# Three pairs in the first and sixth feed-forward stages of a two-block network, early block loads, and a buffer of its own for the last w_out chunk

## The chip, the cores and the metric

One core of a Trainium2 chip runs the whole kernel as one program. The metric is the device time of the execution in microseconds (us); three runs of the kernel before took 2106.66, 2107.87 and 2108.87 us, median 2107.87. Engines are called TensorE (PE in the rows), VectorE (DVE), ScalarE (ACT), GpSimd (POOL) and SyncE (SP, which here only issues DMAs).

## The reference, cut to what matters

One sequence of 256 tokens with 1024 features passes through four layers in float32: two of a first block (mixers HGRN2, then forgetting attention, "fox") and two of a second block (a short convolution, then sparse attention, "nsa", which has a shared key and value stage "kv" in front). Each layer has a feed-forward part before and one behind its mixer, so there are eight, called ffn 0 to ffn 7 here:

```
def swiglu(h, w_in, w_out):                  # w_in (1024, 2*2816), w_out (2816, 1024)
    gate, up = jnp.split(h @ w_in, 2, axis=-1)
    return (jax.nn.silu(gate) * up) @ w_out
x = x + 0.5 * swiglu(rmsnorm(x, g), w_in, w_out)
```

The order of stages is ffn 0, hgrn, ffn 1, ffn 2, fox, ffn 3, ffn 4, conv, ffn 5, kv, ffn 6, nsa, ffn 7.

## The kernel before, in words

*Splits.* Every float32 operand is split into a high and a low part in TensorE's fp32r type, and a product is three matmuls: high by high, high by low, low by high. ScalarE writes the high part (`w_hi`, `wo_hi`, `ht_hi`), VectorE the low one by a subtraction (`w_lo`, `wo_lo`, `ht_lo`). Each piece of weights (128 x 2048 values) goes through both, into a ring of four slots.

*A feed-forward stage.* It starts with the transposition of x (L653), scaled and split into `xt_hi_`, `xt_lo_`. The 2816 hidden features are cut into 11 chunks of 256 (NCH = 11). A plain chunk loads 512 columns of w_in (gate and up, 2 MB, into `raw_in`, L431), and TensorE makes `2 token tiles x 8 slices x 3 = 48` matmuls of 512 columns (L561 to L563). `read(t)` is the silu on ScalarE (L1149) and the gating on VectorE (L1310), which gives h. `turn(c)` transposes h on TensorE (L888) and splits it (`ht_hi`, `ht_lo`), `weights_out(c)` splits 1 MB of w_out (L1108, L1242) that came into `raw_out` (L435), and `second(c)` adds 24 matmuls (L907 to L909) into four PSUM banks. The last two chunks have code of their own (L965 to L967), with w_out split by halves (L1220, L1384).

*Pairs.* A pair takes chunks c and c+1 together by Strassen's scheme in Winograd's form: the 256 tokens x 1024 features by 1024 x 1024 product is seen as 2 x 2 blocks and made with seven products of 12 matmuls (L839 to L841) in place of eight, 84 matmuls for 96. The order is B11, B21, T2, T3, T1, B22, T4. `blocks` are four 1 MB blocks of w_in in the arena (b11, b12, b21, b22, L447); T3 is b12 + b22, made by an accumulating DMA that GpSimd issues (L1042) once b12 has landed; T2, T4 and T1 are sums on VectorE (L1024, L1028, L1033); `dve_x_add` makes four sums of x, which `act_x_sum` and `dve_x_sum` split (S1 to S4, L1050, L1057). The results are combined on VectorE: the gate of the first tile (L1251), p1s (L1271), `up0` (L1280), `up1` (L1287), p1s again (L1288), `up0` again (L1292), and so on. TensorE may start the pair's second product only when h of chunk c-1 has been read out of bank 1, and the plain chunk after a pair only when up0 has been made (L1292).

`PAIRED` says which chunks begin pairs: 4 and 7 in ffn 0; 2, 5 and 8 in ffn 1, 2, 3, 4 and 7; none in ffn 5 and 6.

*What sets the order.* Every engine has one instruction stream, written out by these functions; semaphores tie them. SyncE issues nearly all weight loads in one order: a plain chunk's load waits until the chunk before is split; w_out's load (`out`) waits until the last contents of `raw_out` are split; blocks of the next pair wait until the pair before has used theirs. Where the first pair of a stage follows a mixer (ffn 1, 3, 7), its blocks are asked for behind chunk 0's work, once the mixer's first x is there. In ffn 0 two blocks go behind chunk 1's turn, two behind chunk 2's.

*GpSimd.* Beside T3 it issues the loads of constants, and in ffn 5 it prepares kv: a bias table and compress weights are loaded (L2203 to L2217), the positions are summed (L2231 to L2238), kv0 is zeroed (L2219). In ffn 5's chunk 0 TensorE makes the bias rows (L2269), ScalarE copies and writes them (L2276, L2278). In ffn 6 hidden matmuls (L2324) read the compress weights, the last one also the positions; after it GpSimd loads the bias table (L2254).

## Time and profile before

| | us |
|---|---|
| median of three runs | 2107.87 |
| profiled execution | 2108.13 |
| its span | 2106.8 |
| TensorE busy in it | 2044.6 |
| VectorE, ScalarE busy | 1514.9, 1138.3 |

The profile is of one execution. The span is the time from its first to its last instruction. A matmul's duration is that of its passage through a pipeline, so that the next starts well before its end; how long a run of matmuls takes is read from starts. "Idle before" and a releaser stand in brackets behind a timeline row.

### The profile page before, as it was taken

Reading aid. Unit: us, or ns where it says so; the run is one execution under the profiler, and the core shown is the slowest. Engines: PE = TensorE matmul, PEld = TensorE weight load, DVE = VectorE, ACT = ScalarE, POOL = GpSimd, SP = SyncE. Lnnn points to the kernel's source line nnn. Section 1 sums busy time; section 2 is a strip of 40 time slices with the busy share of each in tenths; the row PEclk is TensorE's granted clock in tenths of the full one; section 3 lists DMA queues with packets and bytes.
Section 4 is the critical chain, followed back from the end, with each engine's and each line's share of the span. In section 5 each row is a group of like instructions: output and inputs, shape, how many; then the busy total and the mean of one; then the engine's idle time right before and its main releaser. Section 6 shows DMA issues by size and latency. Waiting matters only on the chain.

```text
span 2106.8 us, 26202 instructions
## 1 busy us (share of the span) xinstructions
PE 2044.6 (97%) x10287; PEld 1705.5 (81%) x10287; DVE 1514.9 (72%) x1777; ACT 1138.3 (54%) x1417; POOL 93.4 (4%) x130
## 2 busy tenths in 40 slices
PE   8999999999999999999999999999999999989999
...
PEclk9999999999999999999999999999999999999999
...
DMA packets 232955, 377.82 MB, mean 179 GB/s; under 512 B 18766, under 2 KB 129786, under 8 KB 232832
## 3 DMA queue, kind: packets, MB, share of 16 engines
...
q8 instruction: 82, 1.34, 0.3%
...
## 4 chain that ended last, share of the span: by engine, by line
PE 72%; DVE 13%; ACT 6%; DMA 5%; issue 4%; SPq 0%; DVEq 0%; ACTq 0%
PE bank L561 10%; PE bank L563 10%; PE bank L562 10%; PE acc L907 5%; PE acc L909 5%; PE acc L908 5%; DVE w_lo_ L586 3%; DMA raw_in<-ffn_w_in 2%; PE bank L556 2%; PE bank L557 2%; PE bank L558 2%; PE bank L839 2%; PE bank L840 2%; PE bank L841 2%; DMA raw_out<-ffn_w_out 2%
## 5 line engine op out<-in xcount | busy, mean ns | idle before, releaser
L586 DVE TENSOR_TENSOR w_lo_<-raw_in,w_hi_ 128x2048 fp32r<-128x2048 f32 (+1 forms) x265 | 418.6, 1589 | 137.2 <-ACT w_hi_ L576 136.8
L561 PE MATMUL bank<-w_hi_,xt_hi_ 128*128 128x512 f32 x1104 | 444.6, 403 | 6.6 <-DVE arena L1292 2.4
L563 PE MATMUL bank<-w_hi_,xt_lo_ 128*128 128x512 f32 x1104 | 431.4, 391 | 0.0
L562 PE MATMUL bank<-w_lo_,xt_hi_ 128*128 128x512 f32 x1104 | 430.2, 390 | 0.0
L576 ACT ACTIVATE w_hi_<-raw_in 128x2048 fp32r<-128x2048 f32 (+1 forms) x265 | 351.3, 1346 | 82.0 <-DMA raw_in<-ffn_w_in 32.1
L1242 DVE TENSOR_TENSOR wo_lo_<-raw_out,wo_hi_ 128x2048 fp32r<-128x2048 f32 x80 | 183.6, 2296 | 191.7 <-ACT wo_hi_ L1108 191.5
L1007 DVE TENSOR_TENSOR w_lo_<-arena,w_hi_ 128x2048 fp32r<-128x2048 f32 x119 | 270.4, 2285 | 9.0 <-ACT w_hi_ L999 9.0
L999 ACT ACTIVATE w_hi_<-arena 128x2048 fp32r<-128x2048 f32 x119 | 225.5, 1909 | 53.8 <-DVE arena L1033 28.8
L561 PEld LDWEIGHTS bank<-w_hi_,xt_hi_ 128*128 128x128 f32 x1104 | 207.6, 188 | 51.2 <-DVE arena L1292 5.0
L563 PEld LDWEIGHTS bank<-w_hi_,xt_lo_ 128*128 128x128 f32 x1104 | 207.2, 188 | 44.8
L562 PEld LDWEIGHTS bank<-w_lo_,xt_hi_ 128*128 128x128 f32 x1104 | 207.9, 188 | 38.1
L1108 ACT ACTIVATE wo_hi_<-raw_out 128x2048 fp32r<-128x2048 f32 x80 | 153.0, 1912 | 156.9 <-PE acc L909 124.2
L907 PE MATMUL acc<-wo_hi_,ht_hi_ 128*128 128x512 f32 x576 | 226.0, 392 | 3.8 <-DVE ht_lo_ L1237 3.8
L909 PE MATMUL acc<-wo_hi_,ht_lo_ 128*128 128x512 f32 x576 | 225.2, 391 | 0.0
L908 PE MATMUL acc<-wo_lo_,ht_hi_ 128*128 128x512 f32 x576 | 224.9, 390 | 0.0
L907 PEld LDWEIGHTS acc<-wo_hi_,ht_hi_ 128*128 128x128 f32 x576 | 108.6, 188 | 28.6 <-DVE ht_lo_ L1237 4.7
L909 PEld LDWEIGHTS acc<-wo_hi_,ht_lo_ 128*128 128x128 f32 x576 | 108.5, 188 | 22.9
L908 PEld LDWEIGHTS acc<-wo_lo_,ht_hi_ 128*128 128x128 f32 x576 | 108.5, 188 | 22.3
L1149 ACT ACTIVATE silu_<-bank,rstd_ 128x256 f32<-128x256 f32 x108 | 51.1, 473 | 134.7 <-PE bank L563 134.6
L1103 ACT ACTIVATE ht_hi_<-tr 128x512 fp32r<-128x512 f32 x80 | 47.6, 595 | 131.7 <-PE tr L888 113.7
L556 PE MATMUL bank<-xt_hi_,w_hi_ 128*128 128x256 f32 x352 | 101.9, 289 | 2.8 <-DVE xt_lo_ L747 2.8
L557 PE MATMUL bank<-xt_lo_,w_hi_ 128*128 128x256 f32 x352 | 99.6, 283 | 0.0
...
## 6 DMA issues: line engine op xcount, KB each, us to landing
...
arena<-ffn_w_in POOLq DMA_DIRECT2D x17, 1024.0 KB, 14.2
...
```

The source lines that it names most:

```text
L561: mm(o, xt_hi[:, k, tok], wh(k)[:, 0:w], start=first, stop=False)
L562: mm(o, xt_hi[:, k, tok], wl(k)[:, 0:w], start=False, stop=False)
L563: last = mm(o, xt_lo[:, k, tok], wh(k)[:, 0:w], start=False, stop=end)
L576: act.e.activation(g.piece(g.wh, n, half, k), raw, ACT.Copy).then_inc(g.w_hi, 4 if k is None else 1)
L586: dve.e.tensor_tensor(g.piece(g.wl, n, half, k), raw, g.piece(g.wh, n, half, k).bitcast(F32), ALU.subtract).then_inc(g.w_lo, 4 if k is Non ...
L907: mm(o, g.hth[:, at, :], g.oh[:, i, cols], start=(c == 0 and i == 0), stop=False)
L908: mm(o, g.hth[:, at, :], g.ol[:, i, cols], start=False, stop=False)
L909: ins = mm(o, g.htl[:, at, :], g.oh[:, i, cols], start=False, stop=False)
L999: act.e.activation(g.wh[:, op % 4], g.block_of(i), ACT.Copy).then_inc(g.w_hi, 4)
L1007: dve.e.tensor_tensor(g.wl[:, op % 4], g.block_of(i), g.wh[:, op % 4].bitcast(F32), ALU.subtract).then_inc(g.w_lo, 4)
L1108: act.e.activation(g.oh[:], g.raw_out[:], ACT.Copy).then_inc(g.wo_hi, 2)
L1242: dve.e.tensor_tensor(g.ol[:], g.raw_out[:], g.oh[:].bitcast(F32), ALU.subtract).then_inc(g.wo_lo, 2)
```

## The change

The diff changes seven things. (1) `PAIRED` gives ffn 0 three pairs, at 2, 5 and 8, and ffn 5 too. (2) In ffn 0 all four blocks of the first pair are asked for right behind chunk 1's load and w_out's chunk 0. (3) For ffn 7 they are asked for in nsa. (4) The last w_out chunk of each paired stage but ffn 5 goes to a buffer of its own, `raw_last` in the arena, asked for when the last pair's sixth product is done; the next load into `raw_out` no longer waits for it. (5) In a stage's first pair S3's and S1's splits on VectorE move into the chunk before, T1's sum goes ahead of T3's split, and in every pair the split of the next chunk's second half goes behind up0. (6) ffn 7's B11 is split before chunk 0's w_out, as in the others. (7) GpSimd's preparations for kv move behind ffn 5's last pair, the zeroing of kv0 ahead of the positions; the bias rows are made in kv. The memset of hgrn's scores waits for ffn 0's end.

```diff
...
-PAIRED = {f: (2, 5, 8) if f else (4, 7) for f in (0, 1, 2, 3, 4, 7)}
+PAIRED = {f: (2, 5, 8) for f in (0, 1, 2, 3, 4, 5, 7)}
 PAIRS = [(f, c) for f in range(8) for c in PAIRED.get(f, ())]
...
     return f * NCH + c + (f >= 3) + (f >= 7)
+ASIDE = [m_of(f, NCH - 1) for f in PAIRED if f != 5]
+def outs_until(m):
+    return m + 1 - len([a for a in ASIDE if a <= m])
...
         self.up1 = self.masks[:].rearrange("p a b -> p (a b)")[:, 0:CW].bitcast(F32)
+        self.raw_last = self.area(10240, FC // P, D)
         self.silu0 = self.silu_[:].rearrange("p a b -> p (a b)")
+    def last_out(self, f):
+        return self.raw_last if m_of(f, NCH - 1) in ASIDE else self.raw_out
...
     def out(m, dst, src):
-        sp.wait_ge(g.wo_lo, 2 * m)
+        sp.wait_ge(g.wo_lo, 2 * (m - (m - 1 in ASIDE)))
         sp.e.dma_start(dst, src).then_inc(g.landed_out, 16)
...
             def w_out_chunk(c):
+                if m_of(f, c) in ASIDE:
+                    sp.wait_ge(g.prod, PDN[N0[s] + PAIRED[f][-1]] + 6)
+                    sp.e.dma_start(g.raw_last, w_out[c]).then_inc(g.last_in, 16)
+                    return
                 if f == 7 and c == 0:
...
                     chunk(i)
-                if here and f == 0 and c in (1, 2):
-                    for which in ((1, 0), (2, 3))[c - 1]:
+                if here and PAIRED.get(f, (0,))[0] == 4 and c in (1, 2):
+                    for which in ((1,), (0, 2, 3))[c - 1]:
                         block(p, which)
                     todo = 1
-                    if here:
+                    if here and not f:
+                        for which in (1, 0, 2, 3):
+                            block(p, which)
+                    elif here and STAGES[s - 1] != "nsa":
                         sp.wait_ge(g.x_new, 4 * X[s - 1] + 1)
...
             chunk(i)
+        if kind == "nsa":
+            sp.wait_ge(g.ns_ob, NSA_HEADS)
+            for which in (2, 3):
+                block(p, which)
+            sp.wait_ge(g.xt_lo, 16 * U_NSA_O + 16)
+            for which in (1, 0):
+                block(p, which)
     o = g.t["out"].rearrange("o (t p) d -> p (o t) d", p=P)
...
     def weights_out(c):
-        act.wait_ge(g.landed_out, 16 * (m_of(f, c) + 1))
+        act.wait_ge(g.landed_out, 16 * outs_until(m_of(f, c)))
         used_out(c)
...
             p = PAIRS.index((f, c + 1))
-            if before != "S" and f != 7:
+            if before != "S":
                 act_block(g, act, p, B11)
...
                 turn(c - 1)
-                if f == 7:
-                    act_block(g, act, p, B11)
                 act_block(g, act, p, B21)
...
         act.wait_ge(g.second, 20 * f + 18 + i + 1)
-        act.wait_ge(g.landed_out, 16 * (m_of(f, c) + 1))
-        act.e.activation(g.oh[:, i], g.raw_out[:, i], ACT.Copy).then_inc(g.wo_hi, 1)
+        if m_of(f, c) in ASIDE:
+            act.wait_ge(g.last_in, 16 * (ASIDE.index(m_of(f, c)) + 1))
+        else:
+            act.wait_ge(g.landed_out, 16 * outs_until(m_of(f, c)))
+        act.e.activation(g.oh[:, i], g.last_out(f)[:, i], ACT.Copy).then_inc(g.wo_hi, 1)
         act.wait_ge(g.h_turned, 12 * f + c + i + 1)
...
         if first_one:
+            dve_block_sum(g, dve, p, T1)
             dve_block(g, dve, p, T3)
-            dve_block_sum(g, dve, p, T1)
             gate0()
-            dve_x_sum(g, dve, f, A_S3)
-            dve_x_sum(g, dve, f, A_S1)
         else:
...
         dve.e.tensor_tensor(g.p1s, y[:], g.p1s, ALU.add).then_inc(g.st_c, 1)
-        dve_split(g, dve, n + 2, 1)
         dve.wait_ge(g.prod, PDN[n] + 6)
         dve.e.scalar_tensor_tensor(g.up0, a[:], -1.0, g.up0, ALU.mult, ALU.subtract).then_inc(g.st_c, 1)
+        dve_split(g, dve, n + 2, 1)
         dve.wait_ge(g.silu, 22 * f + 2 * c + 2)
...
                 dve_x_sum(g, dve, f, A_S2)
-                if f != 7:
-                    dve_block(g, dve, p, B11)
+                dve_block(g, dve, p, B11)
                 weights_out(c - 1)
+                dve_x_sum(g, dve, f, A_S3)
                 read(0)
                 turn(c - 1)
-                if f == 7:
-                    dve_block(g, dve, p, B11)
                 dve_block(g, dve, p, B21)
+                dve_x_sum(g, dve, f, A_S1)
                 read(1)
+                dve_block_sum(g, dve, p, T3)
                 dve_block_sum(g, dve, p, T2)
...
         dve.wait_ge(g.wo_hi, 2 * m_of(f, c) + i + 1)
-        dve.e.tensor_tensor(g.ol[:, i], g.raw_out[:, i], g.oh[:, i].bitcast(F32), ALU.subtract).then_inc(g.wo_lo, 1)
+        dve.e.tensor_tensor(g.ol[:, i], g.last_out(f)[:, i], g.oh[:, i].bitcast(F32), ALU.subtract).then_inc(g.wo_lo, 1)
         dve.wait_ge(g.ht_hi, 12 * f + c + i + 1)
...
     pool.e.dma_start(g.masks[:], g.t["c_masks"]).then_inc(g.masks_in, 16)
+    pool.wait_ge(g.wo_lo, 2 * NCH)
     pool.e.memset(g.hg_scores[:], 0.0).then_inc(g.hg_zero, 1)
...
     t = g.t
-    for i in range(4):
-        pool.wait_ge(g.x_new, 4 * X[S_FFN[5] - 1] + i + 1)
+    pool.wait_ge(g.prod, PDN[N0[S_FFN[5]] + PAIRED[5][-1]] + 7)
     pool.e.dma_start(g.relb[0:N_BUCKETS], t["rel_bias_2"]).then_inc(g.rel_in, 16)
...
     for kv, w in enumerate((t["cmp_w1_k_2"], t["cmp_w1_v_2"])):
-        pool.wait_ge(g.prod, PDN[N0[S_FFN[5]] + 3 + kv])
         pool.e.dma_start(g.w1[kv * DH:(kv + 1) * DH], w.rearrange("(j d) h -> d j h", d=DH)).then_inc(g.compress_in, 16)
         pool.e.dma_start(g.w2[:, kv], w).then_inc(g.compress_in, 16)
+    pool.e.memset(g.kv0, 0.0).then_inc(g.kv_set, 1)
+    pool.wait_ge(g.kv_set, 6)
+    pool.e.memset(g.vv.rearrange("p a b g d -> p (a b g) d")[:, :, DH:], 1.0).then_inc(g.kv_set, 1)
+    pool.wait_ge(g.kv_set, 7)
     pool_positions(g, pool)
-    pool.e.memset(g.kv0, 0.0).then_inc(g.kv_set, 1)
-    pool.wait_ge(g.kv_set, 7)
-    pool.e.memset(g.vv.rearrange("p a b g d -> p (a b g) d")[:, :, DH:], 1.0).then_inc(g.kv_set, 1)
...
-def pe_bias_slot(g, pe, j):
+def pe_bias(g, pe):
     rb = g.relb[0:REL_ROWS]
-    if j == 8:
-        pe.wait_ge(g.rel_in, 32)
-        pe.wait_ge(g.kv_set, 1)
-        pe.e.matmul(g.accs[0][0:NSA_HEADS, :], rb, g.onehot[0:REL_ROWS], start=True,
-                    stop=True).then_inc(g.kv_rows_mm, 1)
-def act_bias_slot(g, act, j):
-    if j == 8:
-        act.wait_ge(g.kv_rows_mm, 1)
-        act.e.activation(g.rows[0:NSA_HEADS], g.accs[0][0:NSA_HEADS, :], ACT.Copy).then_inc(g.kv_rows, 1)
-        act.wait_ge(g.kv_rows, 1)
-        act.e.dma_start(g.bias_rows.rearrange("c h w -> h c w"),
-                        g.rows[0:NSA_HEADS].unsqueeze(1).to_broadcast([NSA_HEADS, COPIES, REL_W])).then_inc(g.bias_wrote, 16)
+    pe.wait_ge(g.rel_in, 32)
+    pe.wait_ge(g.kv_set, 1)
+    pe.e.matmul(g.accs[0][0:NSA_HEADS, :], rb, g.onehot[0:REL_ROWS], start=True, stop=True).then_inc(g.kv_rows_mm, 1)
+def act_bias(g, act):
+    act.wait_ge(g.kv_rows_mm, 1)
+    act.e.activation(g.rows[0:NSA_HEADS], g.accs[0][0:NSA_HEADS, :], ACT.Copy).then_inc(g.kv_rows, 1)
+    act.wait_ge(g.kv_rows, 1)
+    act.e.dma_start(g.bias_rows.rearrange("c h w -> h c w"),
+                    g.rows[0:NSA_HEADS].unsqueeze(1).to_broadcast([NSA_HEADS, COPIES, REL_W])).then_inc(g.bias_wrote, 16)
...
             j = 2 * (c - 1) + t
+            if (c, t) == (1, 0):
+                pe_bias(g, pe)
             if c == 1:
...
     if i == CMP_BLOCK - 1:
-        pe.wait_ge(g.kv_set, 6)
+        pe.wait_ge(g.kv_set, 8)
         pe.e.matmul(g.accs[3][:, 0:2], g.pe_sum, g.pe_half, start=True, stop=True)
...
                 return
+            if j == 0:
+                act_bias(g, act)
             if j == 3:
...
```

## Rows read from the trace of the kernel before

**Rows 1.** The page: busy time by engine, granted clock in tenths.
```profile
PE 2044.6 (97%) x10287; PEld 1705.5 (81%) x10287; DVE 1514.9 (72%) x1777; ACT 1138.3 (54%) x1417; POOL 93.4 (4%) x130
...
PEclk9999999999999999999999999999999999999999
```

**Rows 2.** Waits of TensorE: us in total, times, longest.
```profile
PE acc L907 <- DVE ht_lo_ L1237: 3.8, 2, 2.1
...
PE acc L965 <- DVE ht_lo_ L1387: 2.8, 6, 1.2
...
PE bank L839 <- DVE silu_ L1251: 2.5, 1, 2.5
PE bank L561 <- DVE arena L1292: 2.4, 6, 0.4
```

**Rows 3.** TensorE timeline, edges of ffn 1 and ffn 5 (start, us, instruction).
```profile
357.63 1.04 PE L653 MATMUL tr<-ident,x_tok 128*128 128x128 f32 x8
540.82 1.03 PE L653 MATMUL tr<-ident,x_tok 128*128 128x128 f32 x8
1350.43 1.03 PE L653 MATMUL tr<-ident,x_tok 128*128 128x128 f32 x8
1359.21 1.03 PE L2269 MATMUL acc<-arena 33*16 33x512 f32 x2
1539.57 0.39 PE L967 MATMUL acc<-wo_hi_,ht_lo_ 128*128 128x512 f32 x1
```

**Rows 4.** Timeline, first pair of ffn 1, TensorE and VectorE.
```profile
403.44 0.48 PE L839 MATMUL bank<-w_hi_,sums_split 128*128 128x512 f32 x1 [0.35 <-DVE w_lo_ L1007]
414.41 0.68 DVE L1292 SCALAR_TENSOR_TENSOR arena<-bank,arena 128x512 f32<-128x512 f32 x1
415.15 0.50 PE L561 MATMUL bank<-w_hi_,xt_hi_ 128*128 128x512 f32 x1 [0.40 <-DVE arena L1292]
```

**Rows 5.** TensorE timeline, last chunks of ffn 1 and ffn 2.
```profile
535.24 0.50 PE L965 MATMUL acc<-wo_hi_,ht_hi_ 128*128 128x512 f32 x1 [0.50 <-DVE ht_lo_ L1387]
...
719.13 0.50 PE L965 MATMUL acc<-wo_hi_,ht_hi_ 128*128 128x512 f32 x1 [1.18 <-DVE ht_lo_ L1387]
```

**Rows 6.** Opening: timeline, windows (busy us, clock, DMA), landings of L447, L1042.
```profile
29.66 0.47 ACT L1149 ACTIVATE silu_<-bank,rstd_ 128x256 f32<-128x256 f32 x1
56.78 0.50 PE L907 MATMUL acc<-wo_hi_,ht_hi_ 128*128 128x512 f32 x1 [1.72 <-DVE ht_lo_ L1237]
...
20.00:25.00 5.00, 5.00 (x24) 3.81 (x22) 4.90 (x9) 4.97 (x9) 0.00 (x0) 1.00 0.74 283
...
35.00:40.00 5.00, 5.00 (x24) 4.14 (x23) 5.00 (x5) 2.25 (x2) 1.34 (x1) 1.00 1.04 386
...
DMA to landing us min/median/max: 5.1/7.7/19.8
...
DMA to landing us min/median/max: 12.2/14.2/14.9
```

**Rows 7.** ffn 7's first pair: timeline, and the window behind the stop.
```profile
1946.59 2.29 DVE L1024 TENSOR_TENSOR arena<-arena 128x2048 f32<-128x2048 f32 x1 [2.76 <-DMA arena<-ffn_w_in]
1959.18 0.77 PE L839 MATMUL bank<-w_hi_,sums_split 128*128 128x512 f32 x1 [2.51 <-DVE silu_ L1251]
...
1959.20:1962.20 3.00, 3.00 (x7) 2.42 (x8) 2.69 (x3) 3.00 (x3) 0.00 (x0) 0.50 0.03 5
```

**Rows 8.** GpSimd's timeline; VectorE's splits in 1423:1467 and in 1500:1535.
```profile
1423.12 0.61 POOL L2231 TENSOR_TENSOR arena<-arena,gains 128x256 f32<-128x256 f32 x1 [9.53 <-DMA arena<-cmp_w_v]
...
1464.57 1.82 POOL L2219 MEMSET arena<- 128x2048 f32 x1
1603.72 4.52 POOL L2254 DMA_DIRECT2D arena<-bias_rows  x8 [137.14 <-PE acc L2324]
...
L586 DVE TENSOR_TENSOR w_lo_<-raw_in,w_hi_ 128x2048 fp32r<-128x2048 f32 x5 | 12.4, 2475 | 2.5 <-ACT w_hi_ L576 2.5
...
L586 DVE TENSOR_TENSOR w_lo_<-raw_in,w_hi_ 128x2048 fp32r<-128x2048 f32 x4 | 9.2, 2288 | 2.0 <-ACT w_hi_ L576 2.0
```

More of the change, by code:

```diff
@@ L161 @@
 ns_csub ns_cexp ns_cp ns_cturned ns_cpt ns_cpv ns_co ns_turned13
-b11_in b12_in b21_in b22_in t3_in st_add st_t3 sa_raw ss_hi ss_lo st_cp st_c masks_in
+last_in b11_in b12_in b21_in b22_in t3_in st_add st_t3 sa_raw ss_hi ss_lo st_cp st_c masks_in
 own_act own_dve own_pool
@@ L335, in kv_views @@
         self.kv0 = self.area(8768, CMP_STRIDE, 2 * GROUPS, T // CMP_STRIDE)
-        self.pe_w1 = [self.area(8768, 2, P), self.area(9792, 2, P)]
+        self.pe_w1 = [self.area(13120, 2, P), self.area(13376, 2, P)]
         self.pe_sum = self.area(10816, P)
@@ L891, in second @@
     def second(c):
-        if c == 0 and f == 5:
+        if c == 0 and f == 6:
             pe.wait_ge(g.kv_rows, 1)
-        elif c == 0 and f == 6:
             pe.wait_ge(g.kv_gelu, 2)
@@ L1970, in act_narrow @@
 def act_narrow(g, act, m, w, f, hi):
-    act.wait_ge(g.landed_out, 16 * (m + 1))
+    act.wait_ge(g.landed_out, 16 * outs_until(m))
     act.wait_ge(g.acc, 4 * f)
@@ L2241, in pool_positions @@
     ins.then_inc(g.kv_set, 1)
-    pool.wait_ge(g.kv_set, 6)
+    pool.wait_ge(g.kv_set, 8)
 def pool_cmp_bias(g, pool):
@@ L3077, in pe_program @@
     pe_conv(g, pe)
-    pe_ffn(g, pe, 5, lambda j: pe_bias_slot(g, pe, j))
+    pe_ffn(g, pe, 5)
     pe_kv(g, pe)
@@ L3094, in act_program @@
     act_conv(g, act)
-    act_ffn(g, act, 5, lambda j: act_bias_slot(g, act, j))
+    act_ffn(g, act, 5)
     act_kv(g, act)
@@ L3113, in dve_program @@
     dve_conv(g, dve)
-    dve_ffn(g, dve, 5, lambda j: None)
+    dve_ffn(g, dve, 5)
     dve_kv(g, dve)
@@ L3130, in pool_program @@
     pool_conv(g, pool)
+    pool_pairs(g, pool, 5)
     pool_kv(g, pool)
```

## The prediction

> **What bounds the kernel now.** I read the page first: TensorE is busy 97% of the span, and its granted clock stands at full nearly everywhere [rows 1]. So time is won only by giving TensorE fewer matmuls, or by closing its few gaps. Second, the table of TensorE's waits [rows 2]: they add up to some 63 us in the whole run, and those that lie in feed-forward stages are small and repeated: six on ht_lo at L1387 (2.8 us, the stage ends), six on the arena at L1292 (2.4 us, the first plain chunk after a stage's first pair), one of 2.5 us on silu_. Third, the timeline at the stage edges, for what a pair is worth [rows 3]. Fourth, close views of one first pair, of two stage ends, of the opening 60 us, of the last stage, and of GpSimd around the kv stage [rows 4 to 8].
>
> **What a pair is worth.** Two plain chunks take 2 x 48 matmuls of 512 columns, a pair 7 x 12 = 84; it saves 12. A run of 24 such matmuls takes 540.82 - 535.24 = 5.58 us [rows 3, 5], 0.2325 us each, so 12 are 2.8 us. (The 0.39 us beside each matmul is its pipelined duration, not its pitch.) The stages show what is left of that. ffn 1, with three pairs, runs from 357.63 to 540.82: 183.2 us. ffn 5, with none, from 1350.43 to 1539.57 + 0.23: 189.4 us, of which the bias matmul at L2269 takes 1.0 (start 1359.21, next product 1360.17): 188.4 bare [rows 3]. ffn 1 holds three gaps of TensorE: 0.35, 0.40 and 0.50 us of idle [rows 4, 5], with slower restarts some 0.5 to 0.6 each, 1.6 together: 181.6 bare. The difference is 6.8 us, 2.3 per pair.
>
> **ffn 5 and kv.** ffn 5 gets three pairs and starts behind a mixer as ffn 1 does (blocks asked for when its x is there). I take ffn 1's bare 181.6, add 0.5 at its end (its last w_out chunk still goes through raw_out) and 0.4 for the wait that I expect in the first pair (next part): 182.5. That is 6.9 less than now. The bias matmul, its copy and the table's write move into kv: +1.0 there, as TensorE works without large gaps in kv. GpSimd's preparations (rel_bias, compress weights, positions) move from the stage's start to behind the last pair's seventh product. After that TensorE has six runs of 24 matmuls, about 33 us, to the stage's end E. GpSimd needs about 5 us to issue; the second compress load made it idle 9.5 us before the first position product, two loads in a row perhaps 21; the positions took 1423.12 to 1464.57, 41.5 us [rows 8]. They end at E - 33 + 5 + 21 + 41 = E + 34. The step that needs them (last hidden matmul) let GpSimd's next load go at 1603.72, E + 64. 30 us of slack hide it; the zeroing of kv0, now ahead of the positions, is ready long before kv. Value taken: 0.
>
> **First pairs, new order on VectorE.** In ffn 1 the sixth product waited (403.44, on w_lo of B22) and the next plain chunk waited (415.15, on up0, which stood at 414.41 behind the 2.28 us split of that chunk's second half) [rows 4]. S3 and S1 (0.68 each) now run in the chunk before, where VectorE idles for ScalarE and TensorE (0.8 and 1.2 us by the timeline), so everything up to B22 comes 1.2 to 1.3 us earlier: w_lo of B22 at 402.0 instead of 403.3, wanted at 402.9. That wait goes. What is late next is T4: up0 must see the fifth product (ends 402.9, VectorE some 0.2 later), 0.68 us, then w_lo of T4, 2.28 us: 406.0, wanted at 405.7. T4 started at about 406.3 before; I book 0.15 us. The second wait goes whole, since up0 is now ahead of the split: 0.56 with its restart. The split then ends at about 415, and its half is read 2.7 us after the chunk's start at 414.6: hidden. 0.7 us per stage, four stages (ffn 1 to 4): -2.8. Bounds: 0 (T4 late by all that B22 gains) and 1.1 each.
>
> **Stage ends.** The last w_out chunk waits today for raw_out, which chunk 9 frees late; ScalarE's copy then holds back ht_hi and ht_lo: 0.50 in ffn 1, 1.18 in ffn 2 [rows 5], 2.8 in six stages [rows 2]. In its own buffer, asked for after the last pair, it lands over 10 us early, and the chain copy 1.06, ht_hi 0.37, ht_lo 0.42 fits beside 12 matmuls. ffn 1 to 4: -2.4; -0.2 each in ffn 0 and ffn 7 is in their sums.
>
> **ffn 7.** T3, the sum that GpSimd's accumulating DMA makes, landed at 1946.59 after VectorE idled 2.76 us for it; TensorE then stopped 2.51 us at 1959.18 and ran at half clock (0.50 granted, 1.2 GHz, after that stop) over the next matmuls [rows 7]: 12 of them took 4.3 us instead of 2.8. With the first pair's blocks asked for during nsa (from about 1900 and 1907), T3 is there near 1925, needed at 1943. Gone: idle 2.5, 0.4, 0.3, 0.4 and 0.2 (that at the end), 1.5 of half clock, 0.7 of restarts: 6.0. ffn 7 has 1 us less room than ffn 1 in front of T2, so I leave 0.2 for T4: -5.8. Bounds -4 and -6.5. The 0.8 on h_tok at its second chunk stays.
>
> **ffn 0.** One pair more: -2.3. Its wait of 1.72 us at 56.78 (chunk 2 landed late behind blocks) goes with its cause, 1.9 with restart [rows 6]; the two first-pair waits and the end as above: -1.3. Against that stands a first pair that comes 35 us earlier. Data: from 20 to 25 us the DMA moved 283 GB/s at a share of 0.74 [rows 6], because the queue ran dry near 24. The blocks, 1 MB each, now queue there: at 380 GB/s 2.8 us each, b12 at 27, b11 at 30, b21 at 33, b22 at 36; T3 is issued at 28 and takes 12.2 to 14.9 us [rows 6]: 41 to 43. ScalarE must now make the four x sums (0.57 each) before the second silu of chunk 0, which ended its wait at 29.66: it comes 2.2 to 2.6 us later, h at 32.9, and TensorE, wanting it at 32.2, waits 0.8. Then ScalarE is free for B11 at 32.3, after the landing. VectorE: B11 to 36.6, w_out 38.8, S3, h, ht_lo 40.5, B21 42.7, S1, second h 43.8. TensorE is done with B11 at 41.6 and may not overwrite the bank before that h: 2.3 us. Then T2 sum, T4 sum and T2's split end at 50.5, wanted at 52.4; B22's at 61.3, wanted 60.8: 0.6; T4 0.2. Together +3.9. Sum of the stage: -2.3 - 1.9 - 1.3 + 3.9 = -1.6. Bounds: no new wait, -5.5; b11 landing after 19.8 us, the slowest of these loads [rows 6], at 38: +6 more, +4.5.
>
> **Sum.** -1.6 (ffn 0) - 2.8 - 2.4 (ffn 1 to 4) - 6.9 (ffn 5) + 1.0 (kv) - 5.8 (ffn 7) = -18.5. The profiled execution took 2108.13 us (span 2106.8), 0.3 above the median 2107.87. 2108.1 - 18.5 = 2089.6 us.
>
> **A rule that speaks against it.** While GpSimd computed the positions, VectorE's splits took 2475 ns on average, against 2288 without it [rows 8]: 0.2 us each, and some ten such operations will meet it in kv and ffn 6, mostly with slack. The Trainium skill (SBUF — State Buffer, "Who interferes with whom") says that a VectorE instruction with two SBUF inputs and a GpSimd instruction that reads SBUF exclude each other, and the later one blocks for the whole instruction. By the row's average the move costs 0 to 2 us, by the rule it can be the price of the fourth rival below.
>
> **Rivals.**
> - *The opening starves.* For it: the DMA is full from 35 us on (386 GB/s) [rows 6] and plain chunk 4's 2 MB now queue beside T3. Against: 6 MB in 17 us are within the rate seen. b11 or T3 6 us late, paid one for one by an idle TensorE: 2089.6 + 6.4 = 2096.
> - *The opening is covered.* VectorE keeps up and ScalarE's x sums fit: 3.9 us of waits shrink to none: 2085.7.
> - *The first pairs gain nothing.* T4 inherits all of B22's wait and later products the chunk's: 2.8 lost in ffn 1 to 4, and 0.9, 0.7 and 0.9 in ffn 0, 5 and 7: 2094.9. For it: VectorE has no idle left from T2's sum to the last split. Against: up0 ahead of the split needs nothing that is late.
> - *GpSimd in the way.* Each of kv's six splits on VectorE waits for one whole position product of 0.61 us [rows 8], and TensorE with it: 3.7 us more, 2093.3. For it: the 2475 ns. Against: that row shows a third of it, and in kv VectorE idles over a microsecond before most splits.
> - *Slower: the positions come too late.* One chain, the compress loads behind three pairs' traffic and then 41.5 us of positions, ends after E + 64. It decides when the loads take over 50 us, and eats the whole gain at 69 us: 2108 and above. For it: it starts some 90 us later in the stage than today. Against: 9.5 us of idle today [rows 8], 14.9 the slowest accumulate.
>
> **Chances.** Forecast 0.62 (own range 2086 to 2093), starved opening 0.12, covered opening 0.12, GpSimd 0.06, first pairs 0.05, late positions 0.03. This kernel's runs lie within 0.1% of each other; 0.2% is what I call no change, 4.2 us. Faster 0.96, same 0.01, slower 0.03. The range of 8 in 10 reaches down to the covered and up to the starved opening: 2085 to 2096.5.
>
> **What would show it.** ffn 5 at 182 to 183 us with 84 matmuls of L839 to L841 per pair; no wait on silu_ in ffn 7, its clock at full; no wait on up0 after first pairs, a small one at the seventh product; none on ht_lo at L1387 except in ffn 5; in ffn 0 a wait of about 2 us at the second product of the first pair, on h. It is wrong if TensorE idles over 6 us between 30 and 70 us, if the hidden matmul waits for kv_set, or if kv grows by over 2 us.

## The result

The changed kernel takes 2095.11 us, the median of 4 runs (2094.11 to 2098.04), against 2108.37 us (2106.66 to 2109.81) for the kernel before in the same session: ratio 0.994, 95% interval [0.9922, 0.9957]. It is faster, and 5.5 us slower than the 2089.6 us forecast, near the upper end of the range. One stage missed by more than that: ffn 5 was to become 6.9 us shorter and became 3.2 us longer, 10.1 us off. Gains elsewhere that no term foresaw hid some of it.

The stages of the profiled executions, each from its first transposition of x to that of the next stage (ffn 7 to the end of its last matmul), in us:

| stage | before | after | predicted | measured |
|---|---|---|---|---|
| ffn 0 | 192.48 | 190.91 | -1.6 | -1.57 |
| ffn 1 to 4 | 737.03 | 730.94 | -5.2 | -6.09 |
| fox | 158.85 | 157.80 | 0 | -1.05 |
| ffn 5 | 191.31 | 194.52 | -6.9 | **+3.21** |
| kv | 32.81 | 33.84 | +1.0 | +1.03 |
| ffn 6 | 212.00 | 209.37 | 0 | -2.63 |
| nsa | 127.40 | 128.26 | 0 | +0.86 |
| ffn 7 | 190.02 | 184.11 | -5.8 | -5.91 |

hgrn and conv did not move (0.01 each), and x arrives 0.3 us earlier. The sum is -12.5, the difference of the spans 2106.8 and 2094.3.

### The profile after

The page's first block and its clock row; they answer to [rows 1]. TensorE shows 48 matmuls fewer, four more pairs of 12 each, and still 97%.

```profile
PE 2035.0 (97%) x10239; PEld 1699.0 (81%) x10239; DVE 1583.3 (76%) x1823; ACT 1162.5 (56%) x1423; POOL 90.3 (4%) x134
...
PEclk9999999999999999999999999999999999989999
```

TensorE's waits (us in total, times, longest), as in [rows 2]. The six waits on ht_lo at stage ends, the six on the arena behind first pairs and the one on silu_ are gone. In their place stand seven on w_lo, one in each stage's first pair, 0.3 at the most, two on h_tok in ffn 0 (1.7, and 0.56 on another line), and one of 7.6 us that no term of the forecast has. The 0.7 on h_tok at L587 is the one in ffn 7 that was to stay.

```profile
PE acc L990 <- DVE ht_lo_ L1263: 7.6, 1, 7.6
...
PE tr L865 <- DVE w_lo_ L1032: 1.9, 7, 0.3
PE bank L865 <- DVE h_tok L1334: 1.7, 1, 1.7
...
PE acc L932 <- DVE ht_lo_ L1263: 1.0, 1, 1.0
PE bank L587 <- DVE h_tok L1334: 0.7, 1, 0.7
```

The timeline of that place, several engines (start, us, instruction; SPq and POOL's DMA rows are issues). Read it from the bottom up. TensorE stops for 7.57 us because VectorE's ht_lo is late; VectorE stands behind its own split of the out weights, that behind ScalarE's copy at 1514.66, and the copy behind the load of out weights 9. Their buffer was free at 1500.25 (1497.96 + 2.29). SyncE was then still issuing w_kv, 16 loads that took it until 1502.8; ScalarE could copy the load behind them at 1514.66, 11.8 us after its issue. GpSimd had asked for 2 MB of compress weights at 1492.55 and 1493.67.

```profile
1486.93 15.85 SPq L443 DMA_DIRECT2D raw_in<-w_kv  x16
1502.83 16.75 SPq L447 DMA_DIRECT2D raw_out<-ffn_w_out  x2
1492.55 1.13 POOL L2238 DMA_DIRECT2D arena<-cmp_w_k  x1 [0.53 <-POOL arena L2235]
1493.67 1.09 POOL L2238 DMA_DIRECT2D arena<-cmp_w_v  x1
1497.96 2.29 DVE L1268 TENSOR_TENSOR wo_lo_<-raw_out,wo_hi_ 128x2048 fp32r<-128x2048 f32 x1 [1.19 <-ACT wo_hi_ L1133]
1514.66 1.91 ACT L1133 ACTIVATE wo_hi_<-raw_out 128x2048 fp32r<-128x2048 f32 x1 [13.26 <-DMA raw_out<-ffn_w_out]
1519.83 0.80 PE L990 MATMUL acc<-wo_hi_,ht_hi_ 128*128 128x512 f32 x1 [7.57 <-DVE ht_lo_ L1263]
```

The same stretch in windows (busy time of PE, PEld, DVE, ACT, POOL, then granted clock, DMA share, GB/s). The DMA engines are busy all the time from 1500 to 1510 and move 183 GB/s, where [rows 6] have 386 at a like share. Behind the stop TensorE runs partly at its lower level, 1.2 GHz: the 12 matmuls from 1519.83 take 5.3 us, where 12 take 2.8 at 2.4 GHz. 7.6 and 2.5 make the 10.1 by which the stage missed its forecast.

```profile
1500.00:1510.00 10.00, 10.00 (x47) 8.26 (x47) 2.85 (x3) 0.48 (x1) 0.00 (x0) 1.00 1.13 183
1510.00:1520.00 10.00, 2.43 (x11) 1.70 (x10) 3.33 (x3) 4.56 (x4) 7.99 (x12) 0.74 0.35 116
1520.00:1530.00 10.00, 10.00 (x36) 7.89 (x37) 5.08 (x5) 3.03 (x5) 9.06 (x13) 0.75 0.85 315
```

The stage edges, which answer to [rows 3]: ffn 1 from 355.73 to 537.73, ffn 5 from 1341.38 to 1535.90.

```profile
355.73 1.04 PE L679 MATMUL tr<-ident,x_tok 128*128 128x128 f32 x8
537.73 1.04 PE L679 MATMUL tr<-ident,x_tok 128*128 128x128 f32 x8
1341.38 1.03 PE L679 MATMUL tr<-ident,x_tok 128*128 128x128 f32 x8
1535.90 2.02 PE L677 MATMUL tr<-diag_,x_tok 128*128 128x128 f32 x16 [1.90 <-DVE diag_ L770]
```

### The profile page after: what moved, and what is told of

It reads as the page before. It is cut to its first block, busy times and chain, and to the rows that moved or that the text cites. A ratio compares the mean times of both kernels' runs of the same rounds, so it can differ in the third digit from the quotient of the medians.

```text
span 2094.3 us, 26216 instructions
## 1 busy us (share of the span) xinstructions
PE 2035.0 (97%) x10239; PEld 1699.0 (81%) x10239; DVE 1583.3 (76%) x1823; ACT 1162.5 (56%) x1423; POOL 90.3 (4%) x134
## 3 DMA queue, kind: packets, MB, share of 16 engines
HBM read 378.72 MB, written 1.57 MB: 182 GB/s over the span
## 4 chain that ended last, share of the span: by engine, by line
PE 82%; DVE 9%; ACT 4%; issue 2%; DMA 2%; SPq 1%; DVEq 0%; ACTq 0%
PE bank L587 9%; PE bank L589 9%; PE bank L588 9%; PE acc L932 6%; PE acc L934 6%; PE acc L933 6%; PE bank L866 3%; PE bank L865 3%; PE bank L867 3%; PE tr L865 3%; PE tr L866 3%; PE tr L867 3%; PE bank L582 2%; PE bank L583 2%; PE bank L584 2%
## 5 line engine op out<-in xcount | busy, mean ns | idle before, releaser
L612 DVE TENSOR_TENSOR w_lo_<-raw_in,w_hi_ 128x2048 fp32r<-128x2048 f32 (+1 forms) x243 | 380.8, 1575 | 119.5 <-ACT w_hi_ L602 119.2
L587 PE MATMUL bank<-w_hi_,xt_hi_ 128*128 128x512 f32 x976 | 394.2, 404 | 3.2 <-DVE xt_lo_ L713 2.4
L589 PE MATMUL bank<-w_hi_,xt_lo_ 128*128 128x512 f32 x976 | 382.1, 391 | 0.0
L588 PE MATMUL bank<-w_lo_,xt_hi_ 128*128 128x512 f32 x976 | 380.9, 390 | 0.0
L602 ACT ACTIVATE w_hi_<-raw_in 128x2048 fp32r<-128x2048 f32 (+1 forms) x243 | 320.1, 1338 | 77.8 <-DMA raw_in<-ffn_w_in 24.0
L1032 DVE TENSOR_TENSOR w_lo_<-arena,w_hi_ 128x2048 fp32r<-128x2048 f32 x147 | 334.5, 2284 | 5.6 <-ACT w_hi_ L1024 5.6
L1024 ACT ACTIVATE w_hi_<-arena 128x2048 fp32r<-128x2048 f32 x147 | 278.8, 1910 | 56.4 <-DVE arena L1049 29.5
L587 PEld LDWEIGHTS bank<-w_hi_,xt_hi_ 128*128 128x128 f32 x976 | 184.0, 189 | 40.0 <-issue 4.8
L589 PEld LDWEIGHTS bank<-w_hi_,xt_lo_ 128*128 128x128 f32 x976 | 183.5, 188 | 39.8
L865 PE MATMUL bank<-w_hi_,sums_split 128*128 128x512 f32 x252 | 100.6, 399 | 0.2 <-DVE silu_ L1277 0.2
L866 PE MATMUL bank<-w_lo_,sums_split 128*128 128x512 f32 x252 | 100.3, 398 | 0.0
```

What stands on the lines that cost most here:

```text
L587: mm(o, xt_hi[:, k, tok], wh(k)[:, 0:w], start=first, stop=False)
L588: mm(o, xt_hi[:, k, tok], wl(k)[:, 0:w], start=False, stop=False)
L589: last = mm(o, xt_lo[:, k, tok], wh(k)[:, 0:w], start=False, stop=end)
L602: act.e.activation(g.piece(g.wh, n, half, k), raw, ACT.Copy).then_inc(g.w_hi, 4 if k is None else 1)
L612: dve.e.tensor_tensor(g.piece(g.wl, n, half, k), raw, g.piece(g.wh, n, half, k).bitcast(F32), ALU.subtract).then_inc(g.w_lo, 4 if k is Non ...
L865: mm(bank[:], hi[:, k], wh[:, k], start=k == 0, stop=False)
```

## The experiments

"Out weights 9" and "10" are the w_out pieces of ffn 5's last two chunks; a load lands when its data can be used. Two theories for ffn 5. **A**: GpSimd's two compress loads, which the change moved behind the last pair, hold back the out weights. **B**: the 16 small-row loads of w_kv ahead of them in SyncE's queue do it. All edits are made on the changed kernel. The stages that moved, from each run's one profiled execution, and the median of the runs that were repeated (e5 to e8 ran once). ffn 5 with the collision as it is took 193.47, 193.91 and 194.52 us in three executions (e5, e8, after), so that a difference of less than 1 us in this stage says nothing:

| run | ffn 0 | ffn 1 | ffn 2 | ffn 3 | ffn 4 | fox | ffn 5 | ffn 6 | nsa | ffn 7 | kernel |
|---|---|---|---|---|---|---|---|---|---|---|---|
| before | 192.48 | 183.19 | 185.83 | 183.04 | 184.97 | 158.85 | 191.31 | 212.00 | 127.40 | 190.02 | 2108.37 |
| after | 190.91 | 182.00 | 183.60 | 181.63 | 183.71 | 157.80 | 194.52 | 209.37 | 128.26 | 184.11 | 2095.11 |
| e1 compress late | 190.41 | 181.76 | 183.58 | 181.64 | 184.09 | 157.77 | 198.15 | 209.55 | 128.40 | 184.06 | 2099.14 |
| e2 out between kv | 190.22 | 181.62 | 183.57 | 181.64 | 183.59 | 157.79 | 191.78 | 209.84 | 128.44 | 184.18 | 2093.55 |
| e3 both | 190.42 | 181.89 | 183.55 | 181.62 | 183.61 | 156.15 | 198.04 | 209.48 | 128.48 | 184.13 | 2099.43 |
| e4 two pairs | 189.96 | 181.94 | 183.60 | 181.61 | 183.73 | 157.82 | 186.91 | 208.40 | 130.79 | 184.07 | 2088.61 |
| e9 compress last | 190.30 | 181.66 | 183.57 | 181.64 | 183.58 | 156.20 | 184.08 | 208.85 | 128.30 | 184.10 | 2083.81 |
| e9 again | 190.71 | 181.68 | 183.61 | 181.65 | 183.56 | 156.23 | 184.21 | 208.12 | 128.57 | 184.13 | 2085.54 |
| e11 long rows | 190.32 | 181.69 | 183.63 | 181.60 | 183.63 | 157.78 | 193.95 | 208.99 | 128.59 | 184.06 | 2093.84 |
| e5 ffn 0 (4, 7) | 189.87 | 181.86 | 183.59 | 181.63 | 185.03 | 159.63 | 193.47 | 209.54 | 127.31 | 184.13 | |
| e10: e9 and e5 | 189.58 | 181.62 | 183.55 | 181.64 | 183.64 | 158.70 | 184.22 | 208.94 | 127.29 | 184.24 | 2084.82 |
| e6 no own buffer | 191.24 | 182.46 | 184.11 | 182.19 | 184.81 | 157.82 | 195.15 | 209.46 | 128.40 | 184.70 | |
| e7 old order | 191.75 | 182.49 | 184.41 | 182.47 | 184.44 | 157.48 | 195.35 | 208.08 | 128.80 | 184.90 | |
| e8 ffn 7 late | 190.22 | 182.36 | 183.57 | 181.63 | 184.16 | 157.74 | 193.91 | 209.43 | 128.60 | 189.12 | |

### e1: the compress loads behind out weights 9

```diff
     pool.wait_ge(g.kv_set, 5)
+    pool.wait_ge(g.landed_out, 16 * outs_until(m_of(5, NCH - 2)))
     for kv, w in enumerate((t["cmp_w1_k_2"], t["cmp_w1_v_2"])):
```

> GpSimd starts the two 1 MB compress loads only when chunk 9 of ffn 5's out weights has landed; nothing else is changed. ffn 5 took 194.5 us with a TensorE wait of 7.6 us. Theory A (the compress loads hold the rings, w_kv's small rows alone do not): the 16 w_kv loads are issued in about 9 us instead of 15.9, out weights 9 are asked for at about 1500.3 instead of 1502.8 and land in 5 to 6 us instead of 11.7, the wait falls below 1 us, and with the clock's restart gone ffn 5 takes 184.5 to 185.5 and the kernel about 2085.5. Theory B (the 16 w_kv loads ahead in the same queue do it): the issue still ends near 1502.8 and the landing stays above 8 us, the wait stays at 5 us or more, ffn 5 takes 191 or more, the kernel 2092 or more. Both by halves: a wait of 3 to 4, ffn 5 near 189.

2099.14 us, ratio to before 0.9947 [0.9932, 0.9962]: no better than the changed kernel's 0.994 [0.9922, 0.9957], and neither theory's number. ffn 5 takes 198.15, 3.6 us more. Its timeline:

```profile
1487.13 9.19 SPq L443 DMA_DIRECT2D raw_in<-w_kv  x16
1500.47 10.95 SPq L447 DMA_DIRECT2D raw_out<-ffn_w_out  x2
1507.44 1.13 POOL L2239 DMA_DIRECT2D arena<-cmp_w_k  x1 [15.22 <-DMA raw_out<-ffn_w_out]
1506.71 1.92 ACT L1133 ACTIVATE wo_hi_<-raw_out 128x2048 fp32r<-128x2048 f32 x1 [5.12 <-DMA raw_out<-ffn_w_out]
1526.05 1.06 ACT L1246 ACTIVATE wo_hi_<-raw_out 128x1024 fp32r<-128x1024 f32 x1 [13.10 <-DMA raw_out<-ffn_w_out]
1529.20 0.80 PE L990 MATMUL acc<-wo_hi_,ht_hi_ 128*128 128x512 f32 x1 [10.83 <-DVE ht_lo_ L1411]
```

Every step of A came true for out weights 9: w_kv is issued in 9.19 us, the load is asked for at 1500.47 and lands at 1506.7, and TensorE does not wait for it. But the compress loads, now sent at 1507.44, met the next load of the same kind, out weights 10, asked for at about 1511: it landed after some 15 us and TensorE stopped for 10.83. Ahead of that load stood only the compress loads, w_kv's small ones were long through: A's mechanism is shown, and its sum was wrong, because I looked at one load and not at the next.

### e2: out weights 9 between the halves of w_kv

```diff
-    def chunk(i):
+    def chunk(i, halves=(0, 1)):
...
-        for half in range(2):
+        for half in halves:
...
+                if before == "S" and (f, c) == (5, NCH - 1):
+                    chunk(i, (0,))
+                    w_out_chunk(c - 1)
+                    chunk(i, (1,))
+                    todo = c
+                    continue
                 if before == "S":
                     chunk(i)
```

> In SyncE's program the load of out weights 9 of ffn 5 goes between the two halves of w_kv instead of behind both; GpSimd's compress loads stay where they are. Theory A (compress loads): out weights 9 are asked for at 1500.3 at the earliest, since their buffer is free only then, and still share the engines with what is left of 2 MB of compress loads: landing in 8 us or more, a wait of 3 to 5 us, ffn 5 at 188 to 191. Theory B (w_kv): with one half of w_kv behind it the load lands in about 5 to 6 us, wait below 1, ffn 5 at 184.5 to 185.5, the kernel about 2085.5.

2093.55 us, 0.9919 [0.9904, 0.9934]. ffn 5 at 191.78, a wait of 5.52. Timeline:

```profile
1498.68 0.37 SPq L447 DMA_DIRECT2D raw_out<-ffn_w_out  x1
1511.23 1.91 ACT L1139 ACTIVATE wo_hi_<-raw_out 128x2048 fp32r<-128x2048 f32 x1 [11.41 <-DMA raw_out<-ffn_w_out]
1516.19 0.80 PE L996 MATMUL acc<-wo_hi_,ht_hi_ 128*128 128x512 f32 x1 [5.52 <-DVE ht_lo_ L1269]
```

The load is asked for as soon as its buffer is free and still takes 12.5 us to land. So the place in SyncE's queue is worth some 2 to 3 us of the stage (by the kernel's ratio it can't be told), and B as the main cause is out: it wanted a landing of 5 to 6 us and a wait below 1. The other half of w_kv, asked for just behind, shared the engines with the load all the same.

### e3: both edits

The two edits above together.

> Both edits together. Either theory: out weights 9 land by 1506, no wait over 1 us, ffn 5 at 184.4 (the value predicted without the collision) to 185.5, the kernel 2085 to 2086. If ffn 5 stays above 187, neither queue order nor the compress loads are the whole cause, and the third pair itself costs something that was not counted.

2099.43 us, 0.9947 [0.9933, 0.9962]; ffn 5 at 198.04. Both theories' forecast failed, for e1's reason: ScalarE's copy of out weights 9 starts at 1504.03, and that of out weights 10 waits 13.81 us for its load.

### e4: two pairs in ffn 5

```diff
-PAIRED = {f: (2, 5, 8) for f in (0, 1, 2, 3, 4, 5, 7)}
+PAIRED = {f: (2, 5) if f == 5 else (2, 5, 8) for f in (0, 1, 2, 3, 4, 5, 7)}
```

> ffn 5 with pairs on chunks 2 and 5 only; chunks 8 to 10 as plain chunks; the compress loads follow the second pair. The collision goes (those loads are out about 50 us earlier, w_kv is asked for behind plain chunks), and one pair's gain of about 2.3 us goes with it. Collision as the whole cause: ffn 5 at 186.5 to 187.5, the kernel 2087 to 2088, faster than the kernel with three pairs. If pairs in this stage were themselves dear: ffn 5 below 185.5.

2088.61 us, 0.9895 [0.9878, 0.9911]. ffn 5 takes 186.91, as forecast from the collision as the whole cause (186.5 to 187.5). The collision itself did not go: out weights asked for at 1450.55, in a stretch without w_kv, land 14 us later beside the compress loads. TensorE does not wait for them; there was room.

```profile
1465.06 1.92 ACT L1133 ACTIVATE wo_hi_<-raw_out 128x2048 fp32r<-128x2048 f32 x1 [1.09 <-DMA raw_out<-ffn_w_out]
```

The run also shows what the third pair is worth in this stage: 186.91 less e9's 184.08 and 184.21 is 2.7 to 2.8, nearly all of its 12 matmuls. The mean of all three there is less, 2.1: the stage before without its bias matmul (190.3) against 184.1.

### e9: the compress loads behind the stage's last out weights

```diff
-    pool.wait_ge(g.landed_out, 16 * outs_until(m_of(5, NCH - 2)))
+    pool.wait_ge(g.landed_out, 16 * outs_until(m_of(5, NCH - 1)))
```

(against e1: one load later.)

> GpSimd starts the two 1 MB compress loads only when ffn 5's last out weights (chunk 10) have landed; nothing else is changed against the changed kernel. If the compress loads beside a wanted out-weights load are the whole cause: both landings take 5 to 6 us again, no wait over 1.5 us on ht_lo in this stage, ffn 5 at 184.4 to 185.5, the kernel about 2085 to 2086, some 10 us below the changed one. The loads are then out at about 1532 and the positions at about 1565, wanted near 1587: no new wait in ffn 6. Rival: the loads now meet w_kv's later chunks (1 MB each, wanted in kv) and kv pays what ffn 5 gains: kv at 40 or more, the kernel near 2092. Second rival: the third pair is dear by itself, ffn 5 above 187.

2083.81 us, 0.9889 [0.9873, 0.9906]. Timeline:

```profile
1484.02 9.15 SPq L443 DMA_DIRECT2D raw_in<-w_kv  x16
1497.36 0.37 SPq L447 DMA_DIRECT2D raw_out<-ffn_w_out  x1
1507.87 0.37 SPq L447 DMA_DIRECT2D raw_out<-ffn_w_out  x1
1513.55 1.13 POOL L2239 DMA_DIRECT2D arena<-cmp_w_k  x1 [24.44 <-DMA raw_out<-ffn_w_out]
1586.31 4.51 POOL L2279 DMA_DIRECT2D arena<-bias_rows  x8 [15.29 <-PE acc L2348]
```

ffn 5 takes 184.08 us, 0.3 from the 184.4 that my terms gave, and kv stays at 33.96, so that the rival that kv pays for it (40 or more) is out, and so is that of a dear third pair (above 187): the two w_kv loads asked for just ahead of the compress loads, 1 MB each, land in time. The positions end 15.29 us before the hidden matmul lets GpSimd go on; the changed kernel had 54.49 us there, so the loads can't go much later. That closes the case: where the 2 MB lie decides 10 us.

> The compress loads behind ffn 5's last out weights, once more, beside the variant with two pairs in ffn 0 and on its chip: 2083 to 2085, ffn 5 at 184.1. fox at 156.2 or 157.8: if it takes different values from run to run of one kernel, its gain against the kernel before belongs to the granted clock and not to the change.

2085.54 us, 0.9885 [0.987, 0.9899]. This is the version that beats both kernels: by some 10 us the changed one, by 1.1% the kernel before.

### e11: the same bytes in long rows

The weights arrive in another order, so this kernel's result is another one; it serves for the time alone.

```diff
-        pool.e.dma_start(g.w1[kv * DH:(kv + 1) * DH], w.rearrange("(j d) h -> d j h", d=DH)).then_inc(g.compress_in, 16)
+        pool.e.dma_start(g.w1[kv * DH:(kv + 1) * DH], w.rearrange("(d j) h -> d j h", d=DH)).then_inc(g.compress_in, 16)
```

> The two compress loads stay where the changed kernel has them, move the same 2 x 1 MB, but read 16 KB in one piece per partition instead of 32 rows of 512 bytes; the weights so arrive in another order, so the compressed keys and values are other numbers (their use takes the same instructions). Theory 1 (short rows: the engines are busy all the time and move only 180 to 230 GB/s): the two loads land in 5 to 7 us, w_kv is issued in about 9 us again, out weights 9 are asked for at 1500.5 and land in 5 to 6 us, the wait of 7.6 us falls below 1, ffn 5 at 184 to 185.5, the kernel near 2084 to 2086. Theory 2 (2 MB more on the rings, whatever the rows, or the two queues against each other): landing of out weights 9 stays above 8 us, ffn 5 at 189 or more.

2093.84 us, 0.9925 [0.9909, 0.9942]. ffn 5 at 193.95, wait 5.91. Timeline:

```profile
1507.25 10.37 SPq L447 DMA_DIRECT2D raw_out<-ffn_w_out  x2
1512.88 1.91 ACT L1133 ACTIVATE wo_hi_<-raw_out 128x2048 fp32r<-128x2048 f32 x1 [11.77 <-DMA raw_out<-ffn_w_out]
```

193.95 lies among the three executions of the unchanged stage: the row length of the compress loads is no main cause, as theory 2 has it, though its landing (above 8 us) did not come. The delay only moved from the landing to the issue: w_kv kept SyncE until 1507.2, and the load behind it then landed in 5.6 us. In this slot 2 MB of GpSimd's and 2 MB of w_kv were asked for together, ahead of 1 MB that was wanted soon. Between 1487 and the landing 5 MB went through in 26 us here and in 28 in the changed kernel. w_kv alone is slow as well: in e1 its 2 MB kept the engines busy from 1487 to about 1498, some 200 GB/s. So are the compress loads: window of e9 in which nothing else moves (180 GB/s at full engines).

```profile
1520.00:1526.00 6.00, 4.21 (x31) 3.62 (x30) 3.46 (x10) 3.73 (x11) 0.00 (x0) 1.00 1.04 180
```

What makes them slow, if not their rows, no run here tells.

### e5 and e10: ffn 0 with pairs on chunks 4 and 7

```diff
-PAIRED = {f: (2, 5, 8) for f in (0, 1, 2, 3, 4, 5, 7)}
+PAIRED = {f: (2, 5, 8) if f else (4, 7) for f in (0, 1, 2, 3, 4, 5, 7)}
```

> ffn 0 alone goes back to two pairs, on chunks 4 and 7, its first pair's blocks asked for behind chunks 1 and 2 as in the kernel before; all else as in the changed kernel. By the prediction's terms that stage without its third pair and without the opening's new waits, but with the new order and its own last buffer: -1.3 against 192.5, so 191.2, perhaps 189.3 if the old wait at the third chunk (1.9) was due to the order of the blocks. Theory 1 (the third pair pays 1.6 net): 191.5 to 192.5. Theory 2 (the opening's waits eat all of the pair's 2.3): 190 to 191, no difference to the changed kernel's 190.2 to 190.9.

> The compress loads behind ffn 5's last out weights, and ffn 0 with two pairs on chunks 4 and 7. ffn 0 at 189.9 (against 190.3 with three pairs), ffn 5 at 184.1, the kernel 2083 to 2084.5: level with the version that has three pairs in ffn 0, if the third pair is eaten by the opening's waits; 1.5 us or more slower if the third pair pays there.

Theory 2. TensorE timeline of e5, the edges of ffn 0:

```profile
9.21 1.97 PE L679 MATMUL tr<-ident,x_tok 128*128 128x128 f32 x8 [3.18 <-DMA x_tok<-x]
...
199.08 1.13 PE L677 MATMUL tr<-diag_,x_tok 128*128 128x128 f32 x8 [1.78 <-DVE diag_ L770]
```

189.87 us, and 189.58 in e10, against 189.96 to 190.91 with three pairs in nine runs: the third pair in ffn 0 brings nothing, or loses some tenths. The opening is not quite that of the kernel before: SyncE asks for one block behind chunk 1 and three behind chunk 2, where it was two and two, and the old wait of 1.72 us is gone here too. e10 takes 2084.82 us, 0.9883 [0.9868, 0.9897], level with e9 beside it (2085.54).

### e6, e7, e8: one part undone each

One execution each; ffn 1 differs by up to 0.4 us between executions of the same code (181.62 to 182.00).

```diff
-ASIDE = [m_of(f, NCH - 1) for f in PAIRED if f != 5]
+ASIDE = []
```

> The last chunk's out weights go through raw_out again in every ffn stage; all else as in the changed kernel. Theory 1 (its own buffer took away the stage-end waits): ffn 1 +0.5, ffn 2 +1.1, ffn 3 and 4 +0.5 each, ffn 0 and 7 +0.2 to 0.4, and six waits on ht_lo at the stage ends come back. Theory 2 (the gain of ffn 1 to 4 is all the first pairs' new order): less than 0.3 in each stage. fox, which gained 1.0 that was not foreseen, stays at 157.8 if that was the clock's phase, and goes back to 158.9 if it hangs on the buffer.

Theory 1: the waits at stage ends are back (row below), and ffn 1, 2, 3 and 7 are longer by 0.46, 0.51, 0.56 and 0.59; ffn 4 by 1.10, but that stage also varies between 183.6 and 185.0 elsewhere (e5, before). fox stays at 157.82.

```profile
PE acc L990 <- DVE ht_lo_ L1411: 2.2, 6, 0.5
```

```diff
         if first_one:
+            dve_block(g, dve, p, T3)
             dve_block_sum(g, dve, p, T1)
-            dve_block(g, dve, p, T3)
             gate0()
+            dve_x_sum(g, dve, f, A_S3)
+            dve_x_sum(g, dve, f, A_S1)
...
+        dve_split(g, dve, n + 2, 1)
         dve.wait_ge(g.prod, PDN[n] + 6)
...
-        dve_split(g, dve, n + 2, 1)
...
-                dve_x_sum(g, dve, f, A_S3)
...
-                dve_x_sum(g, dve, f, A_S1)
...
-                dve_block_sum(g, dve, p, T3)
...
```

(The last line changes nothing: T3's sum is GpSimd's in every pair.)

> VectorE's order in and ahead of first pairs as in the kernel before (S3 and S1 inside the pair, T3's split ahead of T1's sum, the last split ahead of up0); all else as in the changed kernel. Theory 1 (the prediction: 0.7 us per first pair): ffn 1, 3 and 4 at +0.5 to +0.9 each, a wait of 0.3 to 0.4 on w_lo at the sixth product and one of 0.4 on the arena at the next plain chunk in each. Theory 2 (T4 inherits the wait): +0.2 or less each. ffn 0 may lose more, since its first pair is the one without room: +0.5 to +1.5.

Theory 1: ffn 1, 2, 3, 4 and 7 are longer by 0.49, 0.81, 0.84, 0.73 and 0.79; ffn 0 by 0.84. Waits of TensorE:

```profile
PE bank L587 <- DVE arena L1318: 2.8, 7, 0.4
PE bank L865 <- DVE w_lo_ L1032: 2.5, 7, 0.4
```

```diff
-                    elif here and STAGES[s - 1] != "nsa":
+                    elif here:
...
-        if kind == "nsa":
-            sp.wait_ge(g.ns_ob, NSA_HEADS)
-            for which in (2, 3):
-                block(p, which)
-            sp.wait_ge(g.xt_lo, 16 * U_NSA_O + 16)
-            for which in (1, 0):
-                block(p, which)
```

ScalarE's and VectorE's first split of the pair also stand behind the turn again.

> ffn 7's first-pair blocks are asked for when its x is there, as before, and their split on ScalarE and VectorE stands behind the turn again; all else as in the changed kernel. Theory 1 (the late T3 is the whole loss): ffn 7 at 189 to 190 instead of 184.1, with a wait of about 2.5 us at the second product on silu_ and half clock behind it. Theory 2 (half of the gain comes from the new order and the own buffer): ffn 7 at 187 or less.

Theory 1: ffn 7 takes 189.12, +5.0, and the wait on silu_ is back (2.0 us; the other one is ffn 0's):

```profile
PE bank L858 <- DVE silu_ L1272: 2.3, 2, 2.0
```

## Why the forecast was right, and where it was not

**The time: in the range by luck.** It lies in the range of 8 in 10 (2085 to 2096.5), but outside the forecast's own 2086 to 2093. ffn 5 alone missed by 10.1 us, which would have put 2089.6 at 2099.7, above the range. 4.1 us came back from stages where I had booked nothing or less: ffn 6 2.6, fox 1.1, ffn 1 to 4 0.9, x 0.3, ffn 7 0.1, against 0.9 lost in nsa.

**First pairs, -2.8 for ffn 1 to 4: right.** e7 gives 2.87 back in these four stages (0.49 + 0.81 + 0.84 + 0.73); with e6 that is 5.5 of the 6.1 measured. T4 is late as booked: timeline of the changed kernel, ffn 1, 0.27 where I had 0.15.

```profile
404.22 0.47 PE L865 MATMUL tr<-w_hi_,xt_hi_ 128*128 128x512 f32 x1 [0.27 <-DVE w_lo_ L1032]
```

**Stage ends, -2.4: right.** e6 gives 2.6 back in the four, about 0.5 in each of ffn 1 to 3 and 1.1 in ffn 4. ffn 7's own share was 0.6, not 0.2.

**ffn 7, -5.8: right.** Measured -5.9; e8 alone takes 5.0 of it back.

**ffn 0, -1.6: right in its sum and in most of its waits.** Timeline after, in order: the turn of chunk 0 on h (0.8 forecast, 0.56 found), B21 on h (2.3, 1.75), the fourth product, T3, on silu_ (none forecast, 0.22), the seventh, T4, on w_lo (0.2, 0.20). The 0.6 forecast for the sixth, B22, did not come.

```profile
32.85 0.63 PE L914 MATMUL tr<-ident,h_tok 128*128 128x128 f32 x4 [0.56 <-DVE h_tok L1334]
43.42 0.50 PE L865 MATMUL bank<-w_hi_,xt_hi_ 128*128 128x512 f32 x1 [1.75 <-DVE h_tok L1334]
55.40 0.50 PE L865 MATMUL bank<-w_hi_,sums_split 128*128 128x512 f32 x1 [0.22 <-DVE silu_ L1277]
64.34 0.47 PE L865 MATMUL tr<-w_hi_,xt_hi_ 128*128 128x512 f32 x1 [0.20 <-DVE w_lo_ L1032]
```

Of its four terms only -2.3 and +3.9 belong to the third pair, +1.6 together; the old wait and the first-pair terms, -3.2, come without it. e5 bears that out: 2.6 us saved with two pairs, 1.6 to 2.5 with three. So my sum said before the run that the third pair does not pay in this stage, and I did not read it that way: for e5 I set "the third pair pays 1.6 net" first.

**kv, +1.0: right** (+1.03).

**ffn 5: the failed step.** "GpSimd needs about 5 us to issue; the second compress load made it idle 9.5 us before the first position product, two loads in a row perhaps 21 ... 30 us of slack hide it ... Value taken: 0." The chain that I followed was GpSimd's own, and it held: its positions ended 10.5 us behind the stage's last matmul, not 34 (13.2 us of idle and 33.3 of work, for 21 and 41), with 54.49 us of slack at the hidden matmul, not 30. What I left out is that a step that is moved takes its transfers with it; the "0" had no term for them. The two compress loads landed after 10.6 and 15.4 us, in the one stretch of the kernel where SyncE asks for 16 small loads and has a wanted one behind them. The missing term is 10.1 us; without the collision the stage takes 184.1 (e9), 7.2 less than before, against 6.9 forecast. The own buffer for the last out weights, which the other stages have and this one has not, costs little: in e9 TensorE waits 0.28 us for it where I had booked 0.5.

The kernel before shows the pattern in ffn 6, and I passed over it. Timeline there: out weights asked for at 1610.61, 6.9 us behind GpSimd's bias loads ([rows 8], 1603.72), land 17.5 us later, and the in weights behind them later still; the longer of the two waits on ht_lo [rows 2], 2.1 us, hangs on those.

```profile
1610.61 0.37 SPq L435 DMA_DIRECT2D raw_out<-ffn_w_out  x1
1628.15 1.92 ACT L1108 ACTIVATE wo_hi_<-raw_out 128x2048 fp32r<-128x2048 f32 x1 [8.95 <-DMA raw_out<-ffn_w_out]
1632.02 1.92 ACT L576 ACTIVATE w_hi_<-raw_in 128x2048 fp32r<-128x2048 f32 x1 [1.95 <-DMA raw_in<-ffn_w_in]
```

After, the same wait is 0.99 us and the clock over the 3 us behind it 1.00 (0.66 before); in e9 it is 0.42; that is the better part of ffn 6's 2.6. The out weights land as late as before there (17.3 us); the in weights behind them came 0.9 us earlier. Nothing in the change aims at it, and no run tests it alone.

Of the signs that I had named, "ffn 5 at 182 to 183 us" is the one that failed: by that count, to its last matmul, it took 192.6. One reading was off and nothing rests on it: TensorE's waits before add up to 58.8 us, not some 63.

**The rivals.** None took place. The first pairs gained (e7), and the positions were in time. The covered and the starved opening lie on either side of what ffn 0 did. "GpSimd in the way" was priced at 3.7 us: kv took 33.84 us, no more than its +1.0. Timeline after, one of VectorE's splits and the two GpSimd sums beside it:

```profile
1516.58 2.91 POOL L2262 TENSOR_TENSOR arena<-arena 128x128 f32<-128x128 f32 x2
1516.67 2.50 DVE L1268 TENSOR_TENSOR wo_lo_<-raw_out,wo_hi_ 128x2048 fp32r<-128x2048 f32 x1 [13.82 <-ACT wo_hi_ L1133]
```

VectorE loses 0.2 us (2.50, else 2.28), GpSimd nearly 2 (2.91, else 0.99). That is the Trainium skill's exclusion (SBUF — State Buffer, "Who interferes with whom"): whoever comes second waits for the whole instruction. The trace agrees, and here the engine with the short instructions pays: GpSimd's second sum starts only when VectorE's 2.5 us are over. My rival charged VectorE a whole instruction each time, the wrong side.
